# Three seams of a 298-slab matrix chain rebuilt: last tiles by halves, a product moved to the unnormed operand, normed operands spread

## The reference

```python
merged = sum_n sigmoid(xn @ w_gate[n] + b_gate[n]) * (y_n @ w_branch[n])     # n = 0..3
h = h + merged @ w_out
hn = rms_norm(h, norm2_g);  h = h + square(relu(hn @ w_ff1)) @ w_ff2
hg = rms_norm(h, norm3_g);  h = h + sigmoid(hg @ w_ple_gate + b) * (p @ w_ple)
h = rms_norm(h, final_g)
# second block, with c -> (shift, scale, gate) of an adaptive norm
x = rms_norm(h) * (1 + scale) + shift
proj = x @ w_in_2 + b        # mlstm queries and keys (1024 columns), gates, values, attention ...
h = h + gate1 * ((...) @ w_out_2)
x = rms_norm(h) * (1 + scale2) + shift2;   u = silu(x @ w_gate_2) * (x @ w_up_2)
h = h + gate2 * (u @ w_down_2)
```

## Time and profile before

| | us |
|---|---|
| median of 3 runs | 918.73 |
| lowest, highest | 918.30, 921.71 |
| profiled execution | 917.34 |
| its span on the core | 916.0 |
| TensorE busy in it | 897.2 |

### The profile page before, as it was taken

One profiled execution on the slowest core, in us unless ns is written; L12 is line 12 of the kernel. 1 busy time (PEld: TensorE's weight loads), 2 busy tenths in 40 slices (PEclk: granted clock), 3 DMA queues, 4 the chain that ended last, 5 costly groups with the idle time before them and its releaser, 6 DMA issues.

```text
span 916.0 us, 18439 instructions
## 1 busy us (share of the span) xinstructions
PE 897.2 (98%) x7348; PEld 870.9 (95%) x7348; DVE 729.7 (80%) x1150; ACT 569.7 (62%) x828; POOL 1.9 (0%) x9
## 2 busy tenths in 40 slices
PE   8999999999999999999999989999999999999996
PEld 7999989999999999999999989988999999999996
DVE  5778998889997899888875989987789885555554
ACT  6848456676576687654445777667695664544542
POOL 0000000000000000000000000000000000000000
PEclk9999999999999999999999999999999999999998
DMA  8766546455875689988856546653536656666541
GB/s 302 250 189 220 156 142 202 156 169 194 290 252 176 226 306 341 346 315 306 326 167 202 183 155 201 208 165 119 173 123 197 188 171 201 189 194 197 186 160 47
DMA packets 53157, 189.83 MB, mean 207 GB/s; under 512 B 6208, under 2 KB 6736, under 8 KB 52944
## 3 DMA queue, kind: packets, MB, share of 16 engines
q1 hardware_dynamic: 52496, 187.60, 62.1%
q10 hardware_dynamic: 576, 1.05, 0.3%
HBM read 186.53 MB, written 1.05 MB: 205 GB/s over the span
## 4 chain that ended last, share of the span: by engine, by line
PE 86%; DVE 7%; ACT 4%; issue 1%; DMA 1%; ACTq 0%; DVEq 0%
PE bank L1003 25%; PE bank L1005 25%; PE bank L1006 25%; DVE wlo L1041 2%; PE bank L977 2%; PE bank L979 2%; PE bank L978 2%; ACT whi L1853 1%; DVE cv L1118 1%; DMA H<-in_xT 1%; PE bank L712 1%; DVE Alo L1076 1%; PE bank L949 1%; PE bank L952 0%; PE bank L956 0%
## 5 line engine op out<-in xcount | busy, mean ns | idle before, releaser
L1041 DVE TENSOR_TENSOR wlo<-raw,whi 128x1024 fp32r<-128x1024 f32 x297 | 360.4, 1220 | 110.2 <-ACT whi L1853 109.7
L1853 ACT ACTIVATE whi<-raw 128x1024 fp32r<-128x1024 f32 x297 | 312.1, 1057 | 200.3 <-PE bank L1006 185.9
L1003 PE MATMUL bank<-Alo,whi 128*128 128x256 f32 x1376 | 388.0, 282 | 2.5 <-ACT Ahi L1873 1.3
L1005 PE MATMUL bank<-Ahi,wlo 128*128 128x256 f32 x1376 | 382.8, 278 | 0.0
L1006 PE MATMUL bank<-Ahi,whi 128*128 128x256 f32 x1376 | 382.8, 278 | 0.0
L1003 PEld LDWEIGHTS bank<-Alo,whi 128*128 128x128 f32 x1376 | 259.4, 188 | 7.9 <-issue 5.5
L1006 PEld LDWEIGHTS bank<-Ahi,whi 128*128 128x128 f32 x1376 | 259.4, 189 | 0.0
L1005 PEld LDWEIGHTS bank<-Ahi,wlo 128*128 128x128 f32 x1376 | 258.7, 188 | 0.4 <-issue 0.2
L1005 PE MATMUL bank<-Fhi,wlo 128*128 128x256 f32 (+1 forms) x288 | 81.0, 281 | 0.0
L1006 PE MATMUL bank<-Fhi,whi 128*128 128x256 f32 (+1 forms) x288 | 81.0, 281 | 0.0
L1003 PE MATMUL bank<-Flo,whi 128*128 128x256 f32 x256 | 72.2, 282 | 0.0
(11 more groups left out here) (398 smaller groups left out, 1355.7 us busy)
## 6 DMA issues: line engine op xcount, KB each, us to landing
raw<-in_stream SPq DMA_DIRECT2D x298, 512.0 KB, 4.3
araw<-in_ada SPq DMA_DIRECT2D x48, 512.0 KB, 6.0
TB<-in_TB SPq DMA_DIRECT2D x1, 1536.0 KB, 7.0
a8r<-a SPq DMA_DIRECT2D x16, 64.0 KB, 2.9
bc<-in_bc SPq DMA_DIRECT2D x1, 896.0 KB, 6.1
out<-H SPq DMA_DIRECT2D x3, 256.0 KB, 2.2
H<-in_xT ACTq DMA_DIRECT2D x2, 256.0 KB, 6.9
H<-in_xT ACTq DMA_DIRECT2D x1, 512.0 KB, 9.6
```

What stands on the lines that cost most here:

```text
L1003: pe.matmul(os[j], wh, xl, start=k == 0 and (wide or j == 0), stop=False, skip_group_check=not wide)
L1005: pe.matmul(os[j], wl, xh, start=False, stop=False, skip_group_check=not wide)
L1041: v.tensor_tensor(wlo[:, s % NHL, :], raw[:, s % NRAW, :], whi[:, s % NHL, :].bitcast(F32), ALU.subtract).then_inc(*lo_v.up(s))
L1853: a.activation(whi[:, s % NHL, :], raw[:, s % NRAW, :], ACT.Copy).then_inc(*hi.up(s))
```

## The change

At br3 to wo, the last pair is added, split and waited for in halves (tile by tile), the low part of the pair before comes first on VectorE, and one `low_part` moves behind all of it. At pg to mq0 the last pair's product, sum and high parts go by halves too. `mq1` becomes wide and takes the unnormed operand like mq0; all four wide pairs are drained by `fin_b`. The steps of xb, mfin, mconv, A, rope, x4 and zfin get new slabs, and `split_shifted` a longer distance between a tile's scaling and its low part. zu1 goes to bank 6 and the second half of mv to bank 4. After wo2 ScalarE does a small square root, which brings its table in early.

```diff
-WIDE = ("mq0", "zg0", "zu0")
+WIDE = ("mq0", "mq1", "zg0", "zu0")
+SECOND = {("mq0", 0): 4, ("mq0", 1): 5, ("mq1", 0): 3, ("mq1", 1): 7, ("zg0", 0): 4, ("zu0", 0): 5}
-ASIDE = {("gv", 1): 4}
+ASIDE = {("gv", 1): 4, ("mv", 1): 4, ("zu1", 0): 6}
-TURNS = [186, 188, 190, 192]
+TURNS = [186, 190, 192, 193]
+ROPE = (0, 2, 1, 3)
-    "xb": ([], [173, 173, 174, 174, 174], [173, 173, 174, 174]),
+    "xb": ([], [173, 174, 175, 176, 177, 177], [174, 175, 176, 177]),
-    "A": ([183], [177, 178, 181, 186], [175, 178, 180, 184]),
+    "A": ([185], [180, 181, 183, 187], [179, 180, 182, 186]),
-    "rope": ([], [189, 191, 192, 195], []),
+    "rope": ([], [189, 192, 195, 197], []),
-    "mfin": ([], [175], [175]),
-    "mconv": ([], [*range(177, 189)], [180, 183, 186, 189]),
+    "mfin": ([], [173, 175, 177, 178], [174, 176, 178, 179]),
+    "mconv": ([], [*range(179, 188), 188, 188, 189], [182, 185, 188, 190]),
-    "x4": ([], [234, 235, 235, 235, 235], [234, 235, 235, 235]),
-    "zfin": ([], [236, 237, 238], [236, 237]),
+    "x4": ([], [233, 234, 234, 234, 234, 234], [233, 234, 234, 235]),
+    "zfin": ([], [235, 236, 237, 238], [236, 237]),
...
                 if name == "wo":
-                    w.wait_ge(*merge_s.at(k // 2))
-                    w.wait_ge(*merge_v.at("lo", k // 2))
+                    of = (3, k - 6) if k >= 6 else (k // 2,)
+                    w.wait_ge(*merge_s.at(*of))
+                    w.wait_ge(*merge_v.at("lo", *of))
...
-                if name == "mq0":
+                if name in ("mq0", "mq1"):
                     w.wait_ge(*ah_s.at("pg", k))
                     w.wait_ge(*ah_v.at("pg", k))
...
-                for k in range(10):
+                for k in range(12):
+                    if k >= 4:
+                        rest(k - 4)
                     if k < 8:
...
-                    if k >= 2:
-                        rest(k - 2)
...
+                if (name, p) == ("br3", 3):
+                    low_z(2)
+                    w.wait_ge(*drained_v.at(name, p))
+                    for j in range(2):
+                        v.tensor_tensor(mg[:, j, :], mg[:, j, :], g[:, j, :], ALU.add).then_inc(*merge_v.up(name, p, j))
+                    for j in range(2):
+                        w.wait_ge(*merge_s.at(p, j))
+                        v.tensor_tensor(Zlo[1][:, 2 + j, :], merged[:, 6 + j, :], Zhi[1][:, 2 + j, :].bitcast(F32),
+                                        ALU.subtract).then_inc(*merge_v.up("lo", p, j))
+                    return
...
             def fin_b(p):
-                w.wait_ge(*mm.at("mq0", p))
-                bs = [main["mq0", p], banks[4 + p]]
+                of = ("mq0", p) if p < 2 else ("mq1", p - 2)
+                w.wait_ge(*rb_v.at("rb"))
+                w.wait_ge(*mm.at(*of))
+                bs = [main[of], banks[SECOND[of]]]
...
+                    if p == 3:
+                        for j in range(2):
+                            w.wait_ge(*emb_s.at("pg", p, j))
+                            v.tensor_tensor(ple[:, 6 + j, :], ple[:, 6 + j, :], t[:, half(j)], ALU.mult
+                                            ).then_inc(*emb_m.up(p, j))
+                        for j in range(2):
+                            w.wait_ge(*emb_m.at(p, j))
+                            v.tensor_tensor(H[:, 6 + j, :], H[:, 6 + j, :], ple[:, 6 + j, :], ALU.add
+                                            ).then_inc(*res_v.up((name, p, j), (name, p)))
...
-                        if (name, n) in ENDS and ENDS[name, n] >= 1 and name != "pg":
+                        if (name, n) in ENDS and ENDS[name, n] >= 1 and name != "pg" and (name, n) != ("br3", 3):
                             low_part(ENDS[name, n] + 3)
...
-                elif name == "mq1":
-                    w.wait_ge(*mm.at(name, p))
-                    for j in range(2):
-                        k = 4 + 2 * p + j
-                        i = a.activation(mpad[:, k, 3:3 + T], b[:, half(j)], ACT.Identity, bias=col("bmqk", k))
-                    i.then_inc(*drained_s.up((name, p)))
...
                     square("r4", p, t512[0][:, :])
+                    if p == 3:
+                        a.activation(spare, ones[:, 0:1], ACT.Sqrt)
```

More of the change, by code:

```diff
@@ L506, in rope @@
             def rope():
[L508 removed]
+                for n, p in enumerate(ROPE):
                     w.wait_ge(*drained("aqk", p))
[L510 to L511 removed]
+                    if n >= 2:
+                        w.wait_ge(*rope_v.at("done", ROPE[n - 2]))
                     for q in range(4):
                         to, of = slice(32 * q, 32 * q + 32), slice(32 * (q ^ 1), 32 * (q ^ 1) + 32)
[L514 to L515 removed]
+                        sp.dma_start(a8r[n % 2][to, :, :], a8[of, 2 * p:2 * p + 2, :]
+                                     ).then_inc(*turn_in[n % 2].up(p, by=16))
                     yield
@@ L722, in normed @@
                 w.wait_ge(*added.at("A", 3))
+                w.wait_ge(*drained("mq1", 1))
                 for j in range(2):
@@ L729, in ifg_task @@
                 w.wait_ge(*drained("mif", 0))
+                w.wait_ge(*drained("mq1", 0))
                 for tt in range(2):
@@ L900, in ready @@
                     w.wait_ge(*x4_v.at(k))
-                elif NAMES.index(name) > NAMES.index("mq0"):
+                elif NAMES.index(name) > NAMES.index("mq1"):
                     w.wait_ge(*xb_s.at(k))
@@ L990, in tensor_program @@
                     if wide:
-                        second = 5 if (name, p) in (("mq0", 1), ("zu0", 0)) else 4
+                        second = SECOND[name, p]
                         os = [b[:, 0:T + 2], banks[second][:, 0:T + 2]]
-                        w.wait_ge(*(red_v.at(5) if name == "mq0" else ml_s.at("root", 1, 1)))
+                        w.wait_ge(*(red_v.at(5) if name == "mq0" else root.at("r3") if name == "mq1"
+                                    else ml_s.at("root", 1, 1)))
                         if name == "zu0":
@@ L1426, in mconv @@
                 w.wait_ge(*mpad_g.at("set"))
-                for p in range(4):
-                    w.wait_ge(*(fin_s.at(p) if p < 2 else drained("mq1", p - 2)))
+                for p in (0, 2, 1, 3):
+                    w.wait_ge(*fin_s.at(p))
                     for c in range(4):
@@ L1560, in rope @@
             def rope():
-                for p in range(4):
-                    a, r = a8[:, 2 * p:2 * p + 2, :], a8r[p % 2]
+                for n, p in enumerate(ROPE):
+                    a, r = a8[:, 2 * p:2 * p + 2, :], a8r[n % 2]
                     w.wait_ge(*trig_s.at("cos"))
-                    w.wait_ge(*turn_in[p % 2].at(p))
+                    w.wait_ge(*turn_in[n % 2].at(p))
                     for j in range(2):
@@ L1575, in mfin @@
             def mfin():
-                fin_b(0)
-                fin_b(1)
-                yield
+                for p in range(4):
+                    fin_b(p)
+                    yield
             def zfin():
@@ L1647, in fin_b @@
                                         ALU.add)
-                i.then_inc(*drained_v.up(("mq0", p)))
+                i.then_inc(*drained_v.up(of))
             def fin_zg():
@@ L1724, in after_pair @@
                     for j in range(2):
-                        i = v.tensor_tensor(t[:, half(j)], b[:, half(j)], rbc, ALU.mult)
-                    i.then_inc(*drained_v.up((name, p)))
+                        v.tensor_tensor(t[:, half(j)], b[:, half(j)], rbc, ALU.mult
+                                        ).then_inc(*drained_v.up((name, p, j), (name, p)))
                     low_part(ENDS[name, p] + 3)
+                    if p == 3:
[7 more added lines that the diff above has]
+                                            ).then_inc(*res_v.up((name, p, j), (name, p)))
+                        next(tasks["emb"])
+                        return
                     w.wait_ge(*emb_s.at("pg", p))
@@ L2105, in mfin @@
             def mfin():
-                for p in range(2):
-                    w.wait_ge(*drained_v.at("mq0", p))
+                for p in range(4):
+                    w.wait_ge(*(drained_v.at("mq0", p) if p < 2 else drained_v.at("mq1", p - 2)))
                     for j in range(2):
@@ L2188, in after_pair @@
                     q = slice(2 * (p % 2), 2 * (p % 2) + 2)
+                    if p == 3:
+                        for j in range(2):
+                            w.wait_ge(*merge_v.at(name, p, j))
+                            a.activation(Zhi[1][:, 2 + j, :], merged[:, 6 + j, :], ACT.Copy).then_inc(*merge_s.up(p, j))
+                        return
                     w.wait_ge(*merge_v.at(name, p))
@@ L2216, in after_pair @@
                     t = araw[:, p % 3, 0:512]
-                    w.wait_ge(*drained_v.at(name, p))
                     for j in range(2):
-                        i = a.activation(t[:, half(j)], t[:, half(j)], ACT.Sigmoid, bias=col("bple", 2 * p + j))
```

(4 more changed lines are left out.)

32 lines of the change are left out of this document (14 added, 18 removed).

## The result

The changed kernel takes 917.21 us (median of 22 runs, 908.78 to 918.50), the kernel before 919.14 (22 runs, 915.84 to 925.85). The ratio is 0.996, with a 95% interval of 0.9941 to 0.9979. The profiled execution took 916.17 us, of which 914.9 are its span.

What follows compares the result with a forecast made beforehand. TensorE, busy 897.2 of 916.0 us, was taken as the bound, so only its waits or pace could change. The seams' 1.56 + 2.4 + 1.9 = 5.9 us off the median 918.73 gave 912.8, range 910.8 to 920.8.

Steps and rivals of the forecast that it cites:

- case 2: Rival: the last stretch, zu1 to the end of dn, goes at the slow pace; 918.9 us, chance 0.25.
- What bounds the kernel: First step: TensorE, busy 897.2 of 916.0 us; its largest releasers Yhi, 1.4 us, and Ahi, 1.3, belong to the seams.
- Seam 1: br3 to wo: TensorE's wait for pair 2's low part goes, gaining 1.56 us; the moved low part arrives just in time.
- Seam 2: pg to mq0, mq1, mif: shorter or removed waits, less the price of wide matmuls; gain 2.4 us, bounds 1.5 and 2.8.
- (a): At mq0's wait of 0.89 us: working by halves readies the first sum 0.3 us earlier, bounds 0 and 0.5.
- Seam 3: zu0 to zg1 to zu1: early table load and zu1 in bank 6 gain 1.9 us, bounds 1.2 and 2.0.
- The pace: Matmuls start 0.1134 or 0.1176 us apart; which follows without a stop was the largest unknown, 6.1 us in the last stretch.
- case 1: The forecast: seams close, small hitches remain, the last stretch stays fast; 912.8 us, 911.0 to 914.0, chance 0.42.
- case 3: Rival: slow pace in the last stretch and after br3 to wo too, no stop ahead of either; 920.9 us, chance 0.13.
- case 4: Rival: VectorE, with two drains more, falls behind at 550 to 590; 914.3 us, or above 922, chance 0.08.

Runs made afterwards that it cites:

- without the early table: distance 3 without the small square root after wo2, so ScalarE loads its table only when the sum has come; 917.3 us, 0.9984 of before.
- distance 3: Changed kernel with three tiles instead of four between scaling and low part in zg1's normed operand; 910.11 us, 0.9882 of before.
- each seam put back: Two kernels: distance 3 with the br3-to-wo seam as before the change, 912.75 us; distance 3 with the pg-to-mq0, mq1, mif seam as before, 912.36 us.
- pauses: distance 3 with TensorE waiting for GpSimd's answer at six groups of transposes, GpSimd writing to an existing strip; 908.6 us, 0.9899 of before.
- the short matmul: Changed kernel with one extra 64-column matmul ahead of zu1's first, its result overwritten, no wait added; 917.1 us.
- the 4-byte strip: distance 3 with an unused strip of 4 bytes per partition put ahead of the activations; 927.51 us, 1.01 of before.
- the longer one: Kernel of the pauses run with the unused strip ahead of the activations 64 bytes longer; 936.38 us, 1.0197 of before.

## Why the prediction came out as it did

The median of 917.21 lies in the range, and the likeliest case, 912.8, did not come. The second did: the last stretch at the slow pace, forecast at 918.9. That the measured time is so near this is in part luck. On the traced executions case 2 says 917.34 - 5.9 + 6.1 = 917.5, and 916.17 was measured: the seams gave 0.45 less than forecast and the pace cost 0.2 more, but 2 us came from places outside the change (see the ledger).

- **What bounds the kernel.** The prediction calls Yhi's 1.4 us and Ahi's 1.3 the largest waits. The same view has a larger one ahead of them, 2.9 us for whi (L949) at the very start; it lies outside the seams and changes nothing in the sum.
- **Seam 1** had 1.56 and gave 1.65 to 1.67. The moved low part came in time, though by less than the sum had: its terms add to 291.5 for the last Ylo half, not 291.3.
- **Seam 2** had 2.4 and gave 2.3 between the traces of before and after (2.95 where it alone is taken back). Of its pieces (a), the halves at mq0, had 0.3 and gave 0.18. The halves cost what the earlier trace rows had shown, 0.75 and 0.76 for two. The estimate from the Trainium skill's formula in "VectorE: DVE Perf Modes", section "The TRN2 errata — SBUF-src ops pay a fixed extra latency per instruction", is 0.85 for two in a row. The trace agrees with the formula for one (0.42 each), but not with the sum of two, since the second starts 0.34 behind the first.
- **Seam 3** had 1.9 and gave 1.5. Its step had only asked when the first Alo is ready and had set zg1 behind zu0 "at 735.42 and zu1 ... 48 x 0.1134 = 5.4 later". It didn't follow the later tiles, 0.92 us each on VectorE against 0.68 on TensorE. Two of them came late by under 0.1 us. As a term of the sum this is 0.47 us, all that the seam fell short: zu1 began 5.91 behind zg1 and not 5.44, some 0.3 of it the hitches and the rest the slower starts behind them. As the last break ahead of 1440 matmuls it is 6.3.
- **The pace.** That it was the largest unknown, and its price, 6.1, were right (6.3 measured). The choice was wrong: case 1 held that small hitches remain and that the fast pace was also taken at such a one. They remained, and within zg1 they gave the slow pace: 19 of 22 runs here, 11 of 12 without the early table. The hitch that it pointed to, 288.87 in the earlier trace rows, did give the fast pace, in nine of 11 traces; what held there did not hold in zg1, and no view of the trace before could have told. What the trace of before could not show, a passage from wide matmuls with no stop, does leave the fast one: before the first hitch of this kernel, and in 23 of 24 runs of the four kernels that have no hitch there and no new layout (distance 3, each seam put back, pauses). The 24th, 915.98 with seam 1 put back, had the lowest granted clock of its kernel, 0.991, and may belong to them too. So case 1's outcome was to be had, by having no hitch rather than by having one.
- **The slow pace after seam 1 too** (case 3) didn't come in the trace of the changed kernel, which has 0.113. Its mechanism was wrong: the prediction read that the fast stretch behind seam 1 begins at the stop of 291.87, but in that same trace the starts are 0.1134 apart already from the hitch ten matmuls ahead of it, and the change leaves this hitch in place. It can come out slow all the same: the trace with the short matmul, which has the changed seam 1, shows 0.1178 from this hitch on.
- **VectorE falling behind** (case 4) didn't come: between 550 and 590 the trace lists no wait of TensorE, though VectorE is now busy 9.97 of 10 us at 550 to 560.

Three things stay open. Why a hitch of 0.05 to 0.09 in zg1 mostly leaves the slow pace and one of 0.07 at matmul 2225 mostly the fast one, the wait for a bank the fast one in 9 of 12 and 6 of 12 runs, and the transposes nearly always the slow one: the records of the two paces differ in nothing but the distance of the starts. Whether the pauses at the transposes gain on distance 3, or would if they were true stops: there are 1.5 us between medians that were not taken side by side. And how the start addresses set the base pace.

## What to carry to other kernels

On a kernel bound by TensorE, read the distance between starts in every long stretch, not only the waits: here waits of 0.05 us decided over 6 to 7 us, and neither the list of waits nor the idle column names them. Follow the supply of a product's operand tile by tile against the rate at which it is used, since the last tile that comes late counts and not the first. To say where a pace began, look at the starts ahead of a stop as well as behind it: the fast stretch behind seam 1 is ten matmuls older than the stop it seems to follow. When the runs of a kernel fall in two groups, compare group with group and ask what moves runs from one to the other.

## What the runs showed of the hardware

The same 256-column matmul, at a granted clock of 1.00, starts every 0.1134 or 0.1178 us in one layout, every 0.1184 in a second and every 0.1200 in a third. The layouts differ only in how far the activations (Ahi and all behind it) lie from the start of a partition: by the program's own allocation 86080 bytes in both kernels, 86112 with the 4-byte strip (which takes 32), 86144 with the longer one; the weights (whi) stay at 36992. It is no matter of larger multiples being better: 86144 is a multiple of 128 and the slowest.

The Trainium skill, "TensorE: Matmul & The Clock Gate", section "Step-by-step: what each phase is for", says that the loading of the next weights takes no read bandwidth from the running matmul, as the two have ports of their own. The runs don't show what is contended, and none of them tests that statement alone; that the pace depends on where the activations lie beside the weights, it does not explain. The same page, section "Back-to-back issue gap" of the Trainium skill, has a formula that it gives for an isolated matmul, by which 256 columns are an estimated 0.109 us; no long stretch of equal 256-column matmuls here is that fast.

In the layout of both kernels, the pace changes in these eleven traces only where the row of equal matmuls is broken: by a stop, a hitch of 0.05 us or more, transposes, a matmul of another width, and once, near 40 us, by a single start of 0.123 where the next product begins. What a break leaves differs from place to place, and at one and the same place from run to run: the two matmuls over the ones at 500 us, which no edit here touches, leave 0.113 in six of the eleven traces and 0.118 in five.
